# The mixtures' up-projections in two products a block instead of three, gate and up each in a PSUM bank of its own

## What is computed

```python
hid = jax.nn.silu(jnp.einsum('td,edf->tef', t, w1)) * jnp.einsum('td,edf->tef', t, w3)
hid = hid * combine.astype(hid.dtype)[:, :, None]
y = jnp.einsum('tef,efd->td', hid, w2)
```

## Time and profile before

| | |
|---|---|
| median of three runs | 2078.76 us (2073.11 to 2079.86) |
| profiled execution | 2070.91 us, span 2069.1 |
| TensorE busy | 1986.2 us, 96% |
| weight loads | 1942.8 us, 94% |
| VectorE busy | 1446.2 us, 70% |
| ScalarE busy | 1035.8 us, 50% |
| bytes moved | 370.18 MB, 179 GB/s on average |
| products with hh or hl (all stages), L378 to L380 | 3 x 2832, some 278 ns from start to end of one |
| low halves L315 | 590, 1221 ns each |
| roundings L312 | 590, 1047 ns each |

### The profile page before, as it was taken

The page is one execution under the profiler, slowest core; times in us unless marked ns, Lnnn a source line. Parts: engine busy times, 40 slices in busy tenths (PEclk is TensorE's granted clock), DMA queues, the critical chain, the costliest instruction groups (busy, mean ns, idle before and its releaser), DMA issues.

```text
span 2069.1 us, 40471 instructions
## 1 busy us (share of the span) xinstructions
PE 1986.2 (96%) x17190; PEld 1942.8 (94%) x17190; DVE 1446.2 (70%) x2389; ACT 1035.8 (50%) x1480; POOL 8.7 (0%) x17
## 2 busy tenths in 40 slices
PE   7899999999989999999999899999899999999998
PEld 7899999999989899999999889999889999999998
DVE  5867777787578777768756757777759775665554
ACT  5754554544375555545444454444366664444443
POOL 0000000000000000000000000000000000000000
PEclk9999999999999999999999999999999999999999
DMA  6433533697544343348865236788725423365552
GB/s 208 132 114 103 194 113 132 216 321 260 182 143 133 124 158 118 124 173 285 305 203 191 92 109 227 292 310 295 287 90 174 154 94 111 122 202 187 192 193 93
DMA packets 101844, 370.18 MB, mean 179 GB/s; under 512 B 11552, under 2 KB 11936, under 8 KB 101536
## 3 DMA queue, kind: packets, MB, share of 16 engines
q1 hardware_dynamic: 100368, 363.38, 51.7%
q10 hardware_dynamic: 1296, 4.21, 0.6%
HBM read 366.50 MB, written 1.05 MB: 178 GB/s over the span
## 4 chain that ended last, share of the span: by engine, by line
PE 57%; DVE 22%; DMA 9%; ACT 7%; issue 5%; SPq 0%; ACTq 0%; DVEq 0%
PE ps L378 15%; PE ps L380 15%; PE ps L379 15%; DVE low L315 7%; DMA ada_rows<-in_ada 5%; DMA raw<-in_stream 4%; ACT high L312 3%; DVE ada_rows L2107 3%; PE ps L609 1%; DVE sq L3058 1%; PE ps L658 1%; PE ps L2039 1%; PE ps L1599 1%; PE ps L3143 1%; PE ps L912 1%
## 5 line engine op out<-in xcount | busy, mean ns | idle before, releaser
L315 DVE TENSOR_TENSOR low<-raw,high 128x1024 fp32r<-128x1024 f32 x590 | 717.6, 1221 | 368.5 <-ACT high L312 367.5
L378 PE MATMUL ps<-hh,high 128*128 128x256 f32 x2832 | 803.6, 284 | 23.2 <-DVE low L315 16.0
L312 ACT CAST high<-raw 128x1024 fp32r<-128x1024 f32 x590 | 612.7, 1047 | 423.9 <-PE ps L380 324.1
L379 PE MATMUL ps<-hh,low 128*128 128x256 f32 x2832 | 788.4, 278 | 0.0
L380 PE MATMUL ps<-hl,high 128*128 128x256 f32 x2832 | 788.2, 278 | 0.0
L378 PEld LDWEIGHTS ps<-hh,high 128*128 128x128 f32 x2832 | 535.5, 189 | 32.7 <-issue 17.6
L379 PEld LDWEIGHTS ps<-hh,low 128*128 128x128 f32 x2832 | 535.6, 189 | 1.2 <-issue 0.5
L380 PEld LDWEIGHTS ps<-hl,high 128*128 128x128 f32 x2832 | 535.7, 189 | 0.0
L378 PE MATMUL ps<-ffn_high,high 128*128 128x256 f32 x672 | 192.1, 286 | 4.2 <-DVE ffn_low L2126 4.2
L379 PE MATMUL ps<-ffn_high,low 128*128 128x256 f32 x672 | 189.3, 282 | 0.0
L380 PE MATMUL ps<-ffn_low,high 128*128 128x256 f32 x672 | 189.2, 281 | 0.0
(11 more groups left out here) (468 smaller groups left out, 2816.6 us busy)
## 6 DMA issues: line engine op xcount, KB each, us to landing
raw<-in_stream SPq DMA_DIRECT2D x590, 512.0 KB, 4.2
ada_rows<-in_ada SPq DMA_DIRECT2D x96, 512.0 KB, 5.4
c_act<-in_c SPq DMA_DIRECT2D x3, 512.0 KB, 4.3
bias<-in_bias ACTq DMA_DIRECT2D x1, 1536.0 KB, 8.7
xT<-in_xT SPq DMA_DIRECT2D x4, 256.0 KB, 5.6
out<-xT SPq DMA_DIRECT2D x4, 256.0 KB, 2.1
par<-in_par ACTq DMA_DIRECT2D x1, 842.0 KB, 11.2
hybrid_const<-in_const ACTq DMA_DIRECT2D x1, 800.0 KB, 5.9
```

The lines of the kernel that those rows point to most:

```text
L312: return act.copy(self.high[:, slot, :], self.raw[:, slot, :])
L315: return dve.tensor_tensor(self.low[:, slot, :], self.raw[:, slot, :], self.high[:, slot, :].bitcast(F32), ALU.subtract)
L378: pe.matmul(out, sh, mh, start=start, stop=False, **more)
L379: pe.matmul(out, sl, mh, start=False, stop=False, **more)
```

## The change

Gate and up get a PSUM bank each (0 and 1) for every expert, no longer alternating. A block takes two products: the weights' high half over both halves of the input side by side (512 columns, a whole bank), and their low half over the input's high half, added to the first 256 columns. For that the input's halves lie in one buffer, `h_both`. The bank then holds the two parts of the result in its two halves, and they have to be added: ScalarE copies the first half out of PSUM (`copy_gate`, `copy_up`) and VectorE adds the second one to the copy. Silu then works in place in SBUF, and the product of gate and up reads both from SBUF. Before gate of expert s TensorE waits for the addition on gate of expert s - 1, before up for that on up of s - 1; the wait for expert s - 2's product is gone.

```diff
+def wide_products(pe, out, stationary, both, start, stop):
+    sh, sl = stationary
+    pe.matmul(out, sh, both, start=start, stop=False, skip_group_check=True)
+    return pe.matmul(out[:, 0:T], sl, both[:, 0, :], start=False, stop=stop, skip_group_check=True)
...
-        hh = sb("hh", [P, KD, T], dt=F32R)
-        hl = sb("hl", [P, KD, T], dt=F32R)
+        h_both = sb("h_both", [P, 2, KD, T], dt=F32R)
+        hh, hl = h_both[:, 0, :, :], h_both[:, 1, :, :]
...
+            up_sum = sb(f"up_sum_{l}", [P, 2, T], moe)
...
                     def up(s):
-                        if s >= 2:
-                            pe.wait_ge(product_step.sem, product_step.base + s - 1)
                         for m in range(2):
+                            if s:
+                                pe.wait_ge((gate_summed, up_summed)[m].sem, (gate_summed, up_summed)[m].base + s)
                             high_, low_ = w.arrived(pe, up_at(s) + m)
                             for k in range(KD):
                                 if s == m == 0 and k % 2 == 0:
                                     norm.ready(pe, k // 2)
-                                ins = three_products(pe, ps[:, s % 2, m * T:(m + 1) * T],
-                                                     (high_[:, k * P:(k + 1) * P], low_[:, k * P:(k + 1) * P]),
-                                                     (hh[:, k, :], hl[:, k, :]), k == 0, k == KD - 1)
+                                ins = wide_products(pe, ps[:, m, :],
+                                                    (high_[:, k * P:(k + 1) * P], low_[:, k * P:(k + 1) * P]),
+                                                    h_both[:, :, k, :], k == 0, k == KD - 1)
...
+                    def copy_gate(s):
+                        p = s // 2
+                        act.wait_ge(*w.done(up_at(s)))
+                        if p >= PAIRS:
+                            act.wait_ge(hidden_done.sem, hidden_done.base + p - PAIRS + 1)
+                        tell(act.copy(hid[:, p % PAIRS, s % 2, :], ps[:, 0, 0:T]), gate_copied)
+
+                    def copy_up(s):
+                        act.wait_ge(*w.done(up_at(s) + 1))
+                        if s >= 2:
+                            act.wait_ge(product_step.sem, product_step.base + s - 1)
+                        tell(act.copy(up_sum[:, s % 2, :], ps[:, 1, 0:T]), up_copied)
+
                     def silu(s):
                         p = s // 2
-                        act.wait_ge(*w.done(up_at(s) + 1))
-                        if p >= PAIRS:
-                            act.wait_ge(hidden_done.sem, hidden_done.base + p - PAIRS + 1)
-                        tell(act.activation(hid[:, p % PAIRS, s % 2, :], ps[:, s % 2, 0:T], ACT.Silu), silu_done)
+                        act.wait_ge(gate_summed.sem, gate_summed.base + s + 1)
+                        tell(act.activation(hid[:, p % PAIRS, s % 2, :], hid[:, p % PAIRS, s % 2, :], ACT.Silu), silu_done)
...
                         if s < E_N:
+                            copy_gate(s)
                             if s:
                                 w.scalar(act, up_at(s))
...
                             silu(s)
+                            copy_up(s)
                             w.scalar(act, up_at(s) + 1)
...
                     def product(s):
+                        dve.wait_ge(up_copied.sem, up_copied.base + s + 1)
+                        tell(dve.tensor_tensor(up_sum[:, s % 2, :], up_sum[:, s % 2, :], ps[:, 1, T:2 * T], ALU.add), up_summed)
+                        dve.wait_ge(up_summed.sem, up_summed.base + s + 1)
                         dve.wait_ge(silu_done.sem, silu_done.base + s + 1)
                         h_ = hid[:, s // 2 % PAIRS, s % 2, :]
-                        tell(dve.tensor_tensor(h_, h_, ps[:, s % 2, T:2 * T], ALU.mult), product_step)
+                        tell(dve.tensor_tensor(h_, h_, up_sum[:, s % 2, :], ALU.mult), product_step)
...
                     def first_half(s):
+                        dve.wait_ge(gate_copied.sem, gate_copied.base + s + 1)
+                        h_ = hid[:, s // 2 % PAIRS, s % 2, :]
+                        tell(dve.tensor_tensor(h_, h_, ps[:, 0, T:2 * T], ALU.add), gate_summed)
                         w.vector(dve, up_at(s))
```

More of the change, by code:

```diff
@@ L2563, in hybrid_and_moe @@
             signal(n) for n in ("hidden_done", "silu_done", "silu_times_up", "hidden_weighed", "hidden_high"))
+        gate_copied, gate_summed, up_copied, up_summed = (
+            signal(n) for n in ("gate_copied", "gate_summed", "up_copied", "up_summed"))
         PAIRS = 4
```

## The result

The kernel after takes 2099.36 us, median of 3 runs (2092.77 to 2106.01), against 2078.76 before: ratio 1.0095, 95% interval 1.0074 to 1.0117. Run again beside the experiments it took 2102.11 against 2076.15: 1.0116 (1.0083 to 1.0149). So it is about 1% slower, some 20 to 26 us.

The account below looks back on a forecast made before the run. TensorE bounds the kernel, in the first mixture with VectorE's chain close behind. First mixture +13.6 us (start 3.3, even part +10.7, four experts -0.4), second +0.25 (3.25-3.0): +13.9, 2092.6 us on the runs' scale; range 2079 to 2105.

Parts of the forecast that it names:

- TensorE's saving: Up products of both mixtures: wide product 220 ns, 6.7 ns less a block, 0.107 us an expert, 6.8 us in all.
- 384-column row: Profile row of the one 384-column rounded product, 0.18 us: by it a wide product takes 247 ns, a block 20 ns more.
- Rival (d): Wide product 247 ns, a block 20 ns dearer; second mixture loses 9.0 us; 2104.5 us; chance 0.06.
- rival (c): Wide product at a narrow one's price, 113.3 ns; second mixture gains 50 us; some 2046 us; chance 0.02.
- Start of a mixture: Experts 1 to 4: TensorE waits for additions queued behind VectorE's router steps; 3.3 us in the first mixture, 3.25 in the second.
- The first gap: Gate of expert 1: TensorE waits for expert 0's gate addition, behind the router's steps, and starts 2.4 us late.
- stretch of low clock: After the logits, new idle times may bring 1.2 GHz: 0 to 1.7 us a mixture, in the range only.
- Even part, second mixture: Evenly running experts of the second mixture: no addition is awaited, so the products' saving shows, 28 x 0.107 = 3.0 us.
- Even part, first mixture: Experts 7 to 31: gate additions behind VectorE's modulation rows come late; expert 31's gate starts 10.7 us later.
- repeated gaps before gate products: Sign in the first mixture: TensorE gaps of 0.3 to 1.5 us released by the gate addition, expert 31 some 13 us later.
- chain's growth of 8.5 us: First mixture's even part: added copies and additions lengthen VectorE's serial chain by 8.5 us, bounds 3 and 17.3.
- the tighter deadline: First mixture's even part: the gate addition is needed at the next expert's start; 2.2 of the 10.7 us.

Follow-up runs that it names:

- single wide: Changed kernel with three 256-column products a block, except one 512-column product in each mixture (last block of expert 6's up unit); 2091.94 us, one run.
- narrow products: Changed kernel with its banks, waits, copies and additions, but the three 256-column products a block of the kernel before; 2088.69 us, ratio 1.0055 to before.
- Early additions: Changed kernel with copies and additions of experts 0 to 2 put ahead of the router's steps in ScalarE's and VectorE's queues; 2092.39 us, ratio 1.0077.
- grouped: Changed kernel with a unit's eight 512-column products first, then its eight 256-column low-half products; 2094.31 us, ratio 1.0093.
- after again: The changed kernel run once more, unchanged, beside the first experiments; 2102.11 us, ratio 1.0116 to the kernel before.
- Narrow short rows: Changed kernel with three 256-column products a block and VectorE's first-mixture modulation-row work cut to 64 of 1024 columns; 2070.57 us, one run.
- only wide: Changed kernel without the weights' low-half product, so that 512-column products follow one another; 2034.19 us, one run.

## Why the prediction was right in the sum and wrong in a step

Forecast 2092.6 us, range 2079 to 2105, slower at 0.71. Measured 2099.36, slower, inside the range and 6.8 above the forecast. The direction was earned, the nearness was luck, as the sum below shows. The prediction named as a sign of being wrong that the wide product is far from 220 ns, and by this sign its first step failed. By steps, on the profiled pieces:

**TensorE's saving: wrong, sign included.** I took 220 ns for the wide product because I read a narrow product's 113.3 ns as 106.7 for columns and 6.6 "beside them", paid once a product. The runs show twice the time of a narrow product at the same pace: 226 ns where the neighbours take 113.3 (single wide), 234.8 where they take 117.8 (after), and 232.5 to 233 on average in rows of wide ones. So what a product carries beside the clock's columns grows with its columns, and there was nothing to save. The row of ten products of the unrounded type, 215.6 ns, was no bound for it: it is another type. The 384-column row, which pointed to 247, was off by about as much on the other side. The second error was to price the wide product alone. Its narrow companions went from 113.3 to 118.3 ns, and the 24 down products of an expert, which nobody touched, to 117.7. An expert got 16 x (353-340) + 24 x 4.5 = 0.32 us dearer by this (8.24/27 = 0.305 measured), where 0.107 were to be saved. Rival (d), at 0.06, had the second mixture's loss nearly right (9.0 us, measured 8.24), by a price a little too high and without the pace. The Trainium skill's rule that spoke against the change ("TensorE: Matmul & The Clock Gate", section Back-to-back issue gap, 2.5 ns beside the columns of an isolated product) erred the same way: by it the edit would save 2.5 ns a block, and it lost 13. The same section's 131 ns for a sustained product of 512 columns, rival (c), is not borne out for this type: no wide product in any run took less than 225.

**Start of a mixture: right in the mechanism, too small by a fifth.** 3.3 and 3.25 us were forecast; 4.0 and 4.1 came from the last logits product on, and 3.7 and 3.5 with the products of before (narrow). The first gap is the one forecast (2.22 us for 2.4), with the addition behind the router's steps. The second isn't seen as a gap: the expert ran at 1.2 GHz then, and its own slowness filled the time in which the up addition was awaited (1246.54 done, TensorE on at 1246.59). The stretch of low clock that I kept out of the sum as a risk is in both starts of the profile after, 6.8 us each against 3.4 and none before, and largely hidden by that wait: narrow products' second start, with 3.4 us of low clock, took only 0.6 us less. Early additions confirm the queue order as the cause.

**Even part, second mixture**: -3.0 forecast, +8.24 measured, all of it the failed first step. That no addition is awaited there was right: narrow products give 221.33 exactly.

**Even part, first mixture**: right in the mechanism, oversized. +10.7 less 0.4 forecast; with the products of before +7.0 (narrow), with the wide ones +8.0 and +11.1. The repeated gaps before gate products that I named as the sign are there in narrow products, eleven of them; the kernel after has two, as its slower TensorE arrives later. I had written that the loss would come "whatever the products cost". All kernels with additions and whole rows that have every product lie between 230.07 and 234.15, and narrow, grouped and after (230.07, 231.25, 231.03) lie close together: this is why the wide products cost 8.2 us in one mixture and, by the profile after, about 1 in the other (4 by after again). Narrow short rows show that VectorE's rows are what makes the additions late. The chain's growth of 8.5 us counted nearly every addition in full; by the loss of 7.0 less the 2.2 for the tighter deadline it was 4.8, between my bounds.

**Behind the first mixture: a piece that I didn't look at.** I read up to expert 31 and assumed that the lateness there lasts. The kernel before waited 5.3 us just behind it for the same chain, so some was given back: 2.0 us in the profile after (306.10 to 304.13), 1.9 in narrow products; after again, where the wait was 4.2 us, shows none (307.72). The piece also holds stages that nothing touches, whose time differs between executions. With it the first mixture's net price is 5.2 us (narrow), 6.0 (after) and 12.7 (after again).

**Sum.** Forecast 3.3+3.25+10.3-3.0 = +13.9. Measured between the profiles of before and after 4.1+4.2+8.0+8.2-2.0+0.1 = +22.6, and +5.8 from unchanged stages. Narrow products' medians give +12.5 for everything but the products, where the prediction's sum without the products' saving would be 13.9+3.0+0.4 and some 0.6 in the starts (6 experts at 0.107) = +17.9. So the forecast was near by luck, for two errors of opposite sign: the additions cost about 5 us less than forecast, the products about 17 more (13.4 lost for 4.0 saved).

What stays open is what the pace is: why it turns slow behind a wide product, and behind some late narrow products and not behind others, and why one pair of spread products ends it and another doesn't. The runs show that it is neither the clock's level nor the place of the input, and that it lasts where TensorE waits for nothing.

## What to carry to other kernels

Before joining two products into a wider one, measure the wide one on the chip in the stream in which it will run: here 512 columns cost what twice 256 cost or some ns more, and the neighbours became dearer as well. A new result that an earlier engine needs at once turns every queue ahead of it into a deadline; look for the place where the kernel already waits for that queue, also just behind the stretch that you changed. And where two limits lie close together, as TensorE's pace and VectorE's chain in the first mixture, take one away at a time and measure both stretches, or a gain in one will seem to be nothing.

## What the runs showed of the hardware

- Products of the rounded 4-byte type with 256 columns ran at one of two paces, 113.3 or 117.8 ns from start to start, both at a granted clock of 1.00 and with no wait (214 and 206 products in 24 us). A pace lasts for tens of us. In a stream at the fast pace a single product of 512 columns was followed by the slow one (single wide, 1849.62), and so was a late product of 256 columns (before, 1417.72; narrow products, 1375.80 and 1419.80); other late products weren't (narrow products, 1341.38).
- The same kernel takes either pace in stages that no edit touches: from 950 to 1050 us TensorE started 880 products in the profile after (at 113.3 ns up to 1036.73) and 852 in the second profile of the same kernel (at 117.8), at a granted clock of 1.00 both times. Some of the spread between runs (2092.77 to 2106.01) may be this; that it is all of it isn't shown. Two profiles can't be compared piece by piece without looking at the pace first.
- A product of 512 columns took 226 ns at the fast pace and 235 at the slow one, as two of 256 columns do (226.6 and 235.6); in rows of its like it took 232.5 to 233 ns on average, while the down products behind them kept to 113.3 to 113.5 (second mixture of grouped and only wide). Whether its input is one piece or two makes no difference (229.57 us for 27 experts both times).
- The clock fell to its 1.2 GHz level behind the logits' 36-column products with a gap behind them (after, 0.50 from 1242 to 1246 and for 6.8 us in each mixture). Without a gap it fell in the first mixture (early additions, 0.60 from 1238 to 1242; before) and not in the second (early additions, 1.00 from 1803 to 1807).
